# A hybrid attention and SSD layer on one core: second-pass queries, maxima and outputs kept by token's residue of four

## The reference, cut to what matters

```python
DILATED_PATTERNS = ((128, 1), (512, 4), (2048, 16))
h = rms_norm(x, attn_norm_g);  proj = h @ w_in
q, k, v, z, xbc, dt_raw = split(proj)       # 8 query heads, 4 key heads of 64
# attention: for every dilation d the tokens with the same t % d form a sequence; blocks of 128
# queries see their own block and the block before it, under a band mask
m = max(s);  pexp = exp(s - m);  l = sum(pexp);  o = pexp @ v      # per dilation
# the three dilations are merged with the maximum over the three m, then out = num / den
ssm_out = ssd_mixer(z, xbc, dt_raw)         # chunked scan, 16 chunks of 128 tokens, 16 heads
x = x + concat([attn_out, ssm_out]) @ w_out
x = x + conv_ffn(x);  x = x + sigmoid(rms_norm(x) @ w_ple_gate) * (p @ w_ple_proj)
```

## Time and profile before

| what | us |
|---|---|
| median of three runs | 3347.71 |
| the profiled execution | 3352.7 |
| its span, first to last instruction | 3351.0 |
| TensorE busy | 3160.5 (94% of the span) |
| VectorE busy | 1630.4 (49%) |
| ScalarE busy | 818.2 (24%) |
| mean share of the full TensorE clock granted | 0.968 |

### The profile page before, as it was taken

How to read it: one execution, slowest core, us unless ns; L and a number is a source line. 1 busy time by engine, 2 the same in 40 slices (tenths; PEclk the granted TensorE clock), 3 DMA queues, 4 the chain that set the end, 5 groups by cost and what they waited for, 6 DMA issues and landing times. The chain is left out here.

```text
span 3351.0 us, 37968 instructions
## 1 busy us (share of the span) xinstructions
PE 3160.5 (94%) x15525; PEld 2477.0 (74%) x15590; DVE 1630.4 (49%) x1562; ACT 818.2 (24%) x1148; POOL 227.8 (7%) x182
## 2 busy tenths in 40 slices
PE   7899999968988888899899999999999899999899
PEld 5678888745555555678778888888888788788687
DVE  7864552145555543633464554444555532532643
ACT  5221121113343433311311111111111422321421
POOL 0000000003333332000000000000000000000000
PEclk9999999978988999999999999999999999999999
DMA  3222222247465561534311111111111624424542
GB/s 133 94 107 70 75 71 80 75 117 172 129 190 137 164 165 52 189 128 144 136 50 50 41 38 47 50 50 50 50 50 50 220 107 181 158 107 146 153 142 69
DMA packets 228401, 354.90 MB, mean 106 GB/s; under 512 B 38049, under 2 KB 123041, under 8 KB 220737
## 3 DMA queue, kind: packets, MB, share of 16 engines
q1 hardware_dynamic: 224578, 333.39, 31.8%
q0 software_dynamic: 3712, 19.96, 1.6%
HBM read 256.08 MB, written 96.84 MB: 105 GB/s over the span
## 5 line engine op out<-in xcount | busy, mean ns | idle before, releaser
L90 PE MATMUL up_ps<-up_h_hi,up_w_hi 128*128 128x512 f32 x1408 | 550.1, 391 | 7.3 <-DVE up_h_lo L1784 7.3
L91 PE MATMUL up_ps<-up_h_lo,up_w_hi 128*128 128x512 f32 x1408 | 548.7, 390 | 0.0
L92 PE MATMUL up_ps<-up_h_hi,up_w_lo 128*128 128x512 f32 x1408 | 548.7, 390 | 0.0
L90 PE MATMUL inp_ps<-inp_h_hi,carry_q 128*128 128x512 f32 x896 | 353.8, 395 | 12.3 <-DVE inp_h_lo L189 9.5
L91 PE MATMUL inp_ps<-inp_h_lo,carry_q 128*128 128x512 f32 x896 | 349.7, 390 | 0.0
L92 PE MATMUL inp_ps<-inp_h_hi,carry_k_two 128*128 128x512 f32 x896 | 349.6, 390 | 0.0
L90 PEld LDWEIGHTS up_ps<-up_h_hi,up_w_hi 128*128 128x128 f32 x1408 | 265.0, 188 | 64.1 <-issue 9.1
L91 PEld LDWEIGHTS up_ps<-up_h_lo,up_w_hi 128*128 128x128 f32 x1408 | 264.9, 188 | 55.8 <-issue 0.7
L92 PEld LDWEIGHTS up_ps<-up_h_hi,up_w_lo 128*128 128x128 f32 x1408 | 264.8, 188 | 55.0
L1929 DVE TENSOR_TENSOR carry_squares<-up_ps,carry_rows 128x2048 f32<-128x2048 f32 x42 | 96.2, 2292 | 420.8 <-PE up_ps L92 420.4
L90 PE MATMUL down_banks<-down_a_hi,down_w_hi 128*128 128x512 f32 x704 | 277.1, 394 | 14.7 <-DVE down_a_lo L2155 12.4
(11 more groups left out here) (318 smaller groups left out, 4647.4 us busy)
## 6 DMA issues: line engine op xcount, KB each, us to landing
carry_room<-in_w_up_dram SPq DMA_DIRECT2D x42, 512.0 KB, 5.7
act<-carry_room SPq DMA_DIRECT2D x21, 1024.0 KB, 4.6
carry_room<-act SPq DMA_DIRECT2D x7, 2816.0 KB, 13.3
down_a_second<-act SPq DMA_DIRECT2D x7, 2816.0 KB, 18.4
carry_room<-cum_rows SPq DMA_DIRECT2D x16, 1024.0 KB, 6.2
carry_room<-x SPq DMA_DIRECT2D x8, 2048.0 KB, 9.3
carry_room<-in_w_in_dram SPq DMA_DIRECT2D x26, 512.0 KB, 6.0
xbc<-carry_room SPq DMA_DIRECT2D x12, 1024.0 KB, 5.7
```

Source lines behind the costliest of these rows:

```text
L90: pe.matmul(out, w_hi, x_hi, start=first, stop=False)
L91: pe.matmul(out, w_hi, x_lo, start=False, stop=False)
L92: return pe.matmul(out, w_lo, x_hi, start=False, stop=last)
```

## The change

The queries' four tiles are now written to `stage` in another order of tokens: all tokens with t % 4 = 0 first, then those with 1, 2 and 3 (`evacuate_by_residue`). Everything that follows them (normalised high and low parts, `q_two`, `q_max`, the maxima's rows, `exp`'s output for p = 0, `o_den`, the stored numerators and denominators) keeps that order. A block of p = 1 is then contiguous, a block of p = 0 is four runs of 32 (or 64 for two blocks), and one of p = 2 has a step of four.

Pass 1 still wants its queries in token order. So the high part of a query tile is made twice: once put back in token order (`high_by_token`) and stored in a new DRAM tensor `q_by_token`, once by residue. Both use the one buffer `qk_hi`, so ScalarE now takes the root between the two, and VectorE's `low_part` of a query tile comes after the next tile's reciprocal.

SP loads a span of queries as six DMAs of four runs each in place of three. The out-projection loads the attention's part by round and residue, and its split puts the tokens in order again while it rounds. Keys, values and all of pass 1's arithmetic are as before. `both_k_runs` is the mask of p = 0 in the new order. The diff, cut to its core:

```diff
+                if t < QT:
+                    pool.wait_ge(hi_done, 2 * t + 1)
+                    pool.dma_start(q_tok_t[t * P:(t + 1) * P, :], qk_hi.bitcast(F32)).then_inc(hi_stored, 16)
+                pool.wait_ge(hi_done, t + 1 + min(t + 1, QT))
                 pool.dma_start(qk_hi_t[t * P:(t + 1) * P, :], qk_hi.bitcast(F32)).then_inc(hi_stored, 16)
                 pool.wait_ge(lo_done, t + 1)
                 pool.dma_start(qk_lo_t[t * P:(t + 1) * P, :], stage[t % 2]).then_inc(lo_stored[t % 2], 16)
...
+                act.wait_ge(hi_stored, 16 * (t + min(t + 1, QT)))
+                act.activation(qk_hi, stage[t % 2], ACT.Copy).then_inc(hi_done, 1)
+
+            def high_by_token(t):
+                act.wait_ge(normed, t + 1)
                 if t > 0:
-                    act.wait_ge(hi_stored, 16 * t)
-                act.activation(qk_hi, stage[t % 2], ACT.Copy).then_inc(hi_done, 1)
+                    act.wait_ge(hi_stored, 32 * t)
+                act.activation(qk_hi.rearrange("p (m i) -> p i m", i=4), stage[t % 2].rearrange("p (i m) -> p i m", i=4), ACT.Copy
+                               ).then_inc(hi_done, 1)
...
-                if 0 < t <= QKT:
+                if QT < t <= QKT:
                     high(t - 1)
+                elif t > 0 and t <= QT:
+                    high_by_token(t - 1)
                 if t < QKT:
                     act.wait_ge(sum_done, t + 1)
                     act.activation(root, ps[b][:, :], ACT.Sqrt, bias=norm.eps[:, 0:1], scale=1.0 / HD).then_inc(ps_free, 1)
+                    if 0 < t <= QT:
+                        high(t - 1)
...
+            def evacuate_by_residue(t, b):
+                dve.wait_ge(mm_done, t + 1)
+                dve.tensor_tensor(stage[b].rearrange("p (i m) -> p i m", i=4), ps[b][:, :].rearrange("p (m i) -> p i m", i=4),
+                                  norm.rstd[:, :].rearrange("p (m i) -> p i m", i=4), ALU.mult).then_inc(evacuated, 1)
...
             def low_part(t):
-                dve.wait_ge(hi_done, t + 1)
+                dve.wait_ge(hi_done, t + 1 + min(t + 1, QT))
                 dve.tensor_tensor(stage[t % 2].bitcast(F32R), stage[t % 2], qk_hi.bitcast(F32), ALU.subtract).then_inc(lo_done, 1)
...
-                evacuate(t, b, stage[b])
+                if t < QT:
+                    evacuate_by_residue(t, b)
+                else:
+                    evacuate(t, b, stage[b])
                 split(t - b, 0, b)
-                if 0 < t <= QKT:
+                if QT < t <= QKT:
                     low_part(t - 1)
                 if t < QKT:
-                    kind = 0 if t < ATTN // P else 1
+                    kind = 0 if t < QT else 1
                     dve.wait_ge(ps_free, t + 1)
                     dve.reciprocal(root, root).then_inc(inv_done, 1)
+                    if 0 < t <= QT:
+                        low_part(t - 1)
...
+def by_residue(rows, at):
+
+    return rows.rearrange("p (i m) -> p i m", i=4)[:, :, bass.ds(at, P)]
...
+    def block(tile, p, col, blocks=1):
+
+        if p == 0:
+            at = slice(32 * col, 32 * (col + blocks))
+            if len(tile.shape) == 2:
+                return tile.rearrange("p (i m) -> p i m", i=4)[:, :, at]
+            return tile.rearrange("p h (i m) -> p h i m", i=4)[:, :, :, at]
+        first = col * P if p == 1 else col % 4 * 512 + col // 4
+        at = slice(first, first + blocks * P) if p == 1 else slice(first, first + 4 * P - 3, 4)
+        return tile[:, at] if len(tile.shape) == 2 else tile[:, :, at]
+
+    @staticmethod
+    def half(row, p, b):
+
+        if p == 0:
+            return row.rearrange("p (i b a) -> p i b a", i=4, b=2)[:, :, b]
+        return row[:, b * P:(b + 1) * P]
...
+    def both_heads(bank, p, blocks):
+
+        if p == 0 and blocks == 2:
+            return bank.rearrange("p (h i m) -> p h i m", h=2, i=4)
+        if p == 0:
+            return bank.rearrange("p (h i b a) -> p h i b a", h=2, i=4, b=2)[:, :, :, 0]
+        return bank.rearrange("p (h t) -> p h t", h=2)[:, :, 0:blocks * P]
...
+        def span(tile, n):
+            low, high, _ = self.SPANS[n]
+            return tile.rearrange("p (i m) -> p i m", i=4)[:, :, low // 4:high // 4]
...
-            for n, (low, high, _) in enumerate(self.SPANS):
-                at = slice(low, high)
+            for n in range(len(self.SPANS)):
                 if r < KVH - 1:
                     load_keys(r, n)
-                sp.dma_start(self.q_two[0:HD, :, at].bitcast(F32), heads[0][:, :, at]).then_inc(self.q_in[n], 16)
-                sp.dma_start(self.q_two[HD:P, :, at].bitcast(F32), heads[1][:, :, at]).then_inc(self.q_in[n], 16)
-                sp.dma_start(self.q_max[0:HD, :, at].bitcast(F32), heads[0][:, :, at]).then_inc(self.q_in[n], 16)
+                for h in range(2):
+                    for tile, part in ((self.q_two[0:HD, h, :], 0), (self.q_two[HD:P, h, :], 1), (self.q_max[0:HD, h, :], 0)):
+                        sp.dma_start(span(tile.bitcast(F32), n), span(heads[part][:, h, :], n)).then_inc(self.q_in[n], 16)
                 if n == 0 and r > 0:
...
-        dve.tensor_copy(self.m_turn[:, :], self.banks[0:6 * TT, 3, 0:P]).then_inc(self.m_out, 1)
+        rows = [slice(2 * TT * p, 2 * TT * (p + 1)) for p in range(3)]
+        dve.tensor_copy(self.m_turn[rows[0], :].rearrange("c (i a) -> c i a", i=4),
+                        self.banks[rows[0], 3, 0:P].rearrange("c (a i) -> c i a", i=4))
+        dve.tensor_copy(self.m_turn[rows[1], :], self.banks[rows[1], 3, 0:P])
+        dve.tensor_copy(self.m_turn[rows[2], :], self.banks[rows[2], 3, 0:P]).then_inc(self.m_out, 1)
...
-        bank = self.banks[:, 2 + h % 2].rearrange("p (w t) -> p w t", w=2)
+        bank = self.banks[:, 2 + h % 2]
         dve.wait_ge(self.pv_mm, h + 1)
         if j < 8:
             if j == 0 and r > 0:
                 dve.wait_ge(self.den_in, 64 * r)
                 dve.wait_ge(self.o_st, 16 * r)
-            dve.tensor_copy(self.o_den[:, :, self.run(0, 2 * j, 2)], bank).then_inc(self.o_add, 1)
+            dve.tensor_copy(self.block(self.o_den[:, :, :], 0, 2 * j, 2), self.both_heads(bank, 0, 2)).then_inc(self.o_add, 1)
         elif j < 16:
-            into = self.o_den[:, :, self.run(1, 2 * j - TT, 2)]
-            dve.tensor_tensor(into, bank, into, ALU.add).then_inc(self.o_add, 1)
+            into = self.block(self.o_den[:, :, :], 1, 2 * j - TT, 2)
+            dve.tensor_tensor(into, self.both_heads(bank, 1, 2), into, ALU.add).then_inc(self.o_add, 1)
         else:
...
+            out = self.both_heads(self.banks[:, g % 2], p, blocks)
+            mask = (self.both_k_runs[:, :, :, :, :].rearrange("p h i b a -> p (h i b a)") if p == 0
+                    else self.both_k[:, :, :, :].rearrange("p h b t -> p (h b t)"))
+            pe.matmul(out, self.ident_b[:, :], self.both_heads(mask, p, blocks), start=True, stop=False)
+            pe.matmul(out, k_two[:, self.run(p, col, 1)], self.block(self.q_two[:, :, :], p, col, blocks), start=False, stop=False)
+            pe.matmul(out, k_one[0:HD + 1, self.run(p, col, 1)], self.block(self.q_max[:, :, :], p, col, blocks), start=False, stop=True
                       ).then_inc(self.s_mm, 1)
         else:
...
-                pe.matmul(bank[head[e], both], self.v[p][:, col - 1], probs[1][:, e].rearrange("p b t -> p (b t)"), start=True, stop=False)
+                pe.matmul(bank[head[e], both], self.v[p][:, col - 1], probs[1][:, e], start=True, stop=False)
             if has_previous:
                 for e in range(2):
-                    pe.matmul(bank[head[e], first], self.v[p][:, col - 2], probs[0][:, e, 1], start=False, stop=False)
+                    pe.matmul(self.half(bank[head[e], both], p, 0), self.v[p][:, col - 2], self.half(probs[0][:, e], p, 1),
+                              start=False, stop=False)
             for e in range(2):
-                pe.matmul(bank[head[e], second], self.v[p][:, col], probs[2][:, e, 0], start=False, stop=True)
+                pe.matmul(self.half(bank[head[e], both], p, 1), self.v[p][:, col], self.half(probs[2][:, e], p, 0), start=False, stop=True)
...
+        def in_order(tile, k):
+            return tile[:, k].rearrange("p (m i) -> p i m", i=4) if k < KA else tile[:, k]
+
+        def as_it_stands(k):
+            return raw[:, k].rearrange("p (i m) -> p i m", i=4) if k < KA else raw[:, k]
+
...
+                for k in range(first, KA):
+                    for e in range(2):
+                        sp.dma_start(den[64 * e:64 * e + 64, k].rearrange("p (i m) -> p i m", i=4),
+                                     by_residue(den_rows[2 * k + e:2 * k + e + 1, :], col).broadcast_to([64, 4, P])).then_inc(den_in, 16)
+                    sp.dma_start(raw[:, k].rearrange("p (i m) -> p i m", i=4), by_residue(mix_t[k * P:(k + 1) * P, :], col)
+                                 ).then_inc(att_in, 16)
```

(4 more changed lines are left out.)

136 lines of the change are left out of this document (70 added, 66 removed).

## The result

| | before | changed |
|---|---|---|
| median | 3348.37 us (4 executions, the three from before the prediction and one more) | 3379.76 us (4 executions) |
| range | 3346.45 to 3350.16 | 3373.80 to 3381.78 |
| ratio to before | | 1.0091, 95% interval 1.0073 to 1.0108 |
| its profiled execution | 3352.7 | 3373.8 |

The changed kernel is slower by 0.9%, some 31 us (25 to 36), and a second measurement gave 1.0093 (1.0078 to 1.0109). The forecast was 3380. That the number was met does not yet say that its terms were right. Single executions of the changed kernel differ by 8 us, and its profiled one is the fastest of the four, so the two traces are compared by stretches between the same instructions.

The account below looks back on a forecast made before the run. TensorE, busy for 94% of 3351.0 us, and its waits were taken as the bound. In-projection +37.7 and mixers with out-projection -5.4 made +32.3: 3352.7 to 3385.0 profiled, 3380 as median forecast, range 3353 to 3401.

Parts of the forecast that it names:

- low part on the chain: In-projection: the low part stands between reciprocal and scaled product, 2.29 us on the chain, four times, +9.2.
- evacuation waits for the store: In-projection: evacuations of tiles 2 to 5 wait about 3.3 to 3.4 us for the low part's store, +13.6.
- evacuation by residue: In-projection: VectorE's inputs read with a step of four cost 1.72 us per tile, +6.9, bounds 0 and 9.1.
- TensorE's clock: In-projection: idle time ahead of the sums by head slows them by 2.0 us in four turns, +8.0, bounds 0 and 8.
- kept of p = 1's saving: Mixers: contiguous queries save TensorE 23.1 us, two thirds of it kept, -15.4, bounds 0 and 25.
- steps 1 to 4: In-projection: low part behind the reciprocal +9.2, evacuation's wait for the store +13.6, evacuation by residue +6.9, TensorE's clock +8.0.
- step 5: In-projection, ScalarE: the scattered token-order copy may start the root up to 0.1 to 0.9 us late, counted as 0.
- SP's added loads: Mixers: 18 query loads per round, not nine, delay round 3's first addition, +5, and `mix_y` after round 0, +3.
- Rival B: Mixers: queries in runs of 32 slow every full p = 0 step, +27 us, 3407; chance 0.08.
- A: Mixers give nothing back: faster p = 1 products only lengthen waits for `exp`, or strided keys hold the pace; 3395; chance 0.13.
- C: In-projection costs only 22.8 us: the clock stays up or evacuation by residue is free; 3365; chance 0.10.
- D: Faster than before: the mixers return all 38.9 us against the in-projection chain's 22.8 and 6 of SP's delays; 3338; chance 0.09.

Follow-up runs that it names:

- evac_plain: The changed kernel with the queries' evacuation contiguous in token order, all else as changed; 3370.5 us, 1.0069 of the kernel before.
- after_again: The changed kernel measured once more with no edit; 3382.3 us, 1.0093 of the kernel before.
- inproj_alone: The changed kernel's in-projection with the mixers and out-projection of the kernel before; 3388.1 us, 1.0113 of the kernel before.
- mixers_alone: The in-projection of the kernel before with the changed kernel's mixers and out-projection; 3348.8 us, 0.9988 of the kernel before.

## Why the prediction was right, and where it was not

The forecast of 3380 held and so did its two halves in sign: a chain lengthened in the in-projection, a smaller return from the mixers. Against its own terms:

| term | predicted | measured |
|---|---|---|
| low part on the chain | 9.2 | 4 x 2.15 = 8.6 |
| evacuation waits for the store | 13.6 | 2.18 + 2.21 + 2.18 + 2.22 = 8.8 |
| evacuation by residue | 6.9 | 4 x 1.48 = 5.9 |
| TensorE's clock | 8.0 | 9.6, of it 8.3 on tiles 2 to 5 |
| in-projection | 37.7 | 32.9 (sum of these), 32.7 (first trace), 33.3 (means) |
| kept of p = 1's saving | -15.4 | -13.7 in the passes 2 |
| added in the mixers | +5 + 3 + 1 | +3.3 between the passes, the rest at both ends |
| mixers | -6.4 | -9.2 (means) |
| out-projection | +1 | +3.0 (means; not told apart from its levels) |
| phases behind | 0 | +2.3 (means) |

- *Low part behind the reciprocal*: right; the starts 152.19 and 154.33 are its 2.15.
- *The store's wait*: mechanism right, size off by 1.2 per tile. The term took 5.3 to landing from the earlier trace rows; the changed kernel's row says 4.2:

```profile
qk_lo<-carry_room POOLq DMA_DIRECT2D x6, 1024.0 KB, 4.2
```

  Before, the low part's store left right after the high part's, as both came out of one turn; now it leaves alone, 12 us later. That this is the reason for the faster landing was not tried.
- *Evacuation by residue*: the step of four costs 1.65 times, a little less than scaled from the addition of the earlier trace rows; evac_plain and the rows agree.
- *Clock*: right in place and kind. The extra time of the stretch from evacuation to reciprocal, less the evacuation's own, was 1.7, -0.4, 2.3, 2.7, 1.7 and 1.6 for tiles 0 to 5, together 9.6. Tiles 2 to 5, the four turns of the prediction, make 8.3 of it, and 8.4 and 9.5 in the two other traces (after_again, inproj_alone). Tile 1 paid nothing, having been slow before. Tile 0 was slower too, but that may be no part of the change: mixers_alone has the in-projection of before and the same idle time there as the earlier trace rows, and its sums were slow.

```profile
72.01 5.33 PE L531 MATMUL inp_ps<-inp_squares,inp_by_head 128*128 128x512 f32 x8 [2.40 <-ACT inp_squares L404]
```

- *p = 1 on TensorE*: the step of 0.71 is as forecast. Over the mixers' stretch TensorE's busy time is 549.6 with the old mixers (mean of 3 traces) and 533.6 with the new (mean of 5), 16 less and not 23; its waits rose from 93.6 to 99.8, of which those for `exp` from 42.2 to 47.1. Within the passes 2 the change brings 13.7, and undoing TensorE's part alone takes 12.3 of it away: 53 to 59% of the 23.1, a little under the two thirds of the forecast. At the end of the mixers 9 to 11 are left.
- *Upper bound of the phase*: the bounds of steps 1 to 4 add up to 39.9, and to 43.5 with the root's 0.9 of step 5 in four turns; the prediction's "about 42" is neither.
- *SP's added loads*, +5 and +3: wrong. The first wait grew by 1.1 in the mean and not by 5, the second by 2.0. SP's delay itself came as counted: before, the output's first store (`mix_den_fold`) was issued at 1226.84, 1.1 after round 2's last addition; in the changed kernel at 1253.64, 6.6 after it. But the large store behind it then landed sooner. Its row among the DMA issues (count, size, median us from issue to landing), before and in the changed kernel:

```profile
mix_t<-mix_o_den SPq DMA_DIRECT2D x4, 1024.0 KB, 11.1
...
mix_t<-mix_o_den SPq DMA_DIRECT2D x4, 1024.0 KB, 6.6
```

  The step that failed is that the queue's 5.4 go onto the wait in full, as if the time to landing stayed the same. Why the store lands sooner was not tried. What is left of the delay does not reach the later additions: the third addition of round 3 comes 23.9 to 26.5 after the last of round 2 with the old loads and 24.0 to 24.8 with the new, so of "+5, bounds 0 and 8" the lower bound holds. That PSUM's spare bank takes the delay up, as the prediction had it for that bound, fits, but was not tested by itself. After round 0 the stretch between the passes grew by 0.3 in the mean, in place of the 3. The largest growth, 2.0 between rounds 1 and 2, has no term in the prediction, and its cause is open.

So the main mechanisms were right, and the closeness of the number is in part luck. Of the +32.3, the in-projection was put 4 too high (mostly the store's landing) and the mixers 3 too high (too much for SP's loads, partly offset by too much kept). Some 5 came from the out-projection's levels and the phases behind it, for which the sum had 1, and these made up for much of it. Rival B (runs of 32) fell with p = 0 at 0.69, A with the passes 2, C with the clock, D with the in-projection's 33.

The rule of the Trainium skill, page "SBUF — State Buffer", section "Door 1: The DMA port swizzle (why `[64,N]` ≈ `[32,N]`)", that a step of up to 4 fp32 is free, is contradicted again by three pairs of rows, with and without the step: 1.14 and 0.71 on TensorE, 1119 and 689 ns on VectorE, and 3.87 and 1.89 on ScalarE.

## What to carry to other kernels

Before an instruction is moved in a serial chain over several engines, ask whether it stands in a gap now: the low part cost nothing ahead of the reciprocal and 2.2 per tile behind it, and moved the store that frees a buffer onto the path as well. A reordering belongs on the engine with idle time in that phase: the same permutation cost 33 us where it lengthened the chain and none where ScalarE made it in its idle time. A saving in a phase with fixed order and cross-engine waits is not to be counted in full: of 23 us of shorter steps, 14 came off the passes and 9 off the phase. And when a queue gets longer, the time from issue to landing is to be read again as well: 5.5 us more of issuing made a wait 1.1 longer.
